# Row sums by way of DRAM, value tiles copied in SBUF, and late sums folded on VectorE, in the first layer of a two-layer backbone

## What is computed

```python
m = jax.nn.silu(cond) @ w_mod + b_mod            # shift, scale, gate
h = x * (1.0 + sc) + sh
q, k, v, z = jnp.split(h @ w_in[l], 4, axis=-1)
s = jnp.concatenate([s_loc.reshape(b, h, GRID_W, n_win), s_ctx], axis=-1)
p = jax.nn.softmax(s, axis=-1).astype(v.dtype)
y = einsum('bhwij,bhiwjd->bhwd', p_loc, v_win) + einsum('bhwc,bhcd->bhwd', p_ctx, vc)
out = (y * jax.nn.silu(z)) @ w_out[l]
x_new = _layer_norm(DEEPNORM_ALPHA * x + (1.0 + g) * out, ln_g[l], ln_b[l])
```

## Time and profile before

| | |
|---|---|
| median of 3 runs | 1820.04 us (1819.77 to 1820.56) |
| the profiled execution | 1819.72 us, span 1817.9 us |
| PE busy | 1781.4 us (98%), 10525 matmuls |
| PE weight loads busy | 1541.5 us (85%) |
| DVE busy | 1260.0 us (69%), 2268 instructions |
| ACT busy | 925.2 us (51%), 1680 instructions |
| POOL busy | 268.3 us (15%) |
| granted PE clock | 0.998 of full |
| DMA | 124.92 MB, 69 GB/s |

### The profile page before, as it was taken

How to read it: one execution, slowest core, us unless ns; L and a number is a source line. 1 busy time by engine, 2 the same in 40 slices (tenths; PEclk the granted TensorE clock), 3 DMA queues, 4 the chain that set the end, 5 groups by cost and what they waited for, 6 DMA issues and landing times. The chain is left out here.

```text
span 1817.9 us, 30832 instructions
## 1 busy us (share of the span) xinstructions
PE 1781.4 (98%) x10525; PEld 1541.5 (85%) x10525; DVE 1260.0 (69%) x2268; ACT 925.2 (51%) x1680; POOL 268.3 (15%) x219
## 2 busy tenths in 40 slices
PE   7999999999999999989999999999999999999998
PEld 4898989888888888878878988888888888898886
DVE  6677776867677767774877576584848485756758
ACT  2555555565555656570045556464737465554500
POOL 3200000000000000165441010100001010102951
PEclk9999999999999999999999999999999999999999
DMA  9312121212222221234511010101010000101343
GB/s 347 87 52 86 45 85 40 79 54 75 61 75 61 58 78 49 88 96 162 189 70 36 13 46 4 42 12 46 12 35 23 35 23 14 44 12 45 101 154 119
DMA packets 73663, 124.92 MB, mean 69 GB/s; under 512 B 41312, under 2 KB 41472, under 8 KB 73488
## 3 DMA queue, kind: packets, MB, share of 16 engines
q1 hardware_dynamic: 68496, 106.48, 18.3%
q0 software_dynamic: 2384, 8.39, 1.7%
q10 hardware_dynamic: 2736, 9.44, 1.3%
HBM read 106.54 MB, written 17.73 MB: 68 GB/s over the span
## 5 line engine op out<-in xcount | busy, mean ns | idle before, releaser
L522 PE MATMUL acc<-h_hi,w_hi 128*128 128x512 f32 (+1 forms) x1408 | 524.5, 373 | 2.3 <-DVE w_lo L505 1.1
L522 PE MATMUL acc<-h_hi,w_lo 128*128 128x512 f32 (+1 forms) x1408 | 508.7, 361 | 0.0
L522 PE MATMUL acc<-h_lo,w_hi 128*128 128x512 f32 (+1 forms) x1408 | 508.1, 361 | 0.0
L522 PEld LDWEIGHTS acc<-h_hi,w_lo 128*128 128x128 f32 x1408 | 265.5, 189 | 41.5
L522 PEld LDWEIGHTS acc<-h_hi,w_hi 128*128 128x128 f32 x1408 | 265.9, 189 | 39.1 <-DVE h_lo L447 3.6
L522 PEld LDWEIGHTS acc<-h_lo,w_hi 128*128 128x128 f32 x1408 | 266.4, 189 | 33.6
L1649 DVE TENSOR_REDUCE stats<-acc 128x1 f32<-128x1280 f32 x128 | 189.6, 1487 | 43.5 <-PE acc L1756 42.8
L1559 ACT ACTIVATE far_prob<-acc,stats 128x1280 f32<-128x1280 f32 x128 | 170.1, 1329 | 28.3 <-DVE stats L1649 26.6
L1566 ACT ACTIVATE far_pt<-acc 128x512 f32<-128x512 f32 (+1 forms) x192 | 101.0, 526 | 162.6 <-PE acc L1765 159.2
L1756 PE MATMUL acc<-k_dup,q_stack 128*128 128x512 f32 (+1 forms) x768 | 176.9, 367 | 1.8 <-ACT far_prob L1559 0.4
L1160 ACT ACTIVATE near_pt_hi<-acc 128x384 fp32r<-128x384 f32 (+1 forms) x208 | 110.4, 531 | 122.6 <-PE acc L1347 104.4
(11 more groups left out here) (207 smaller groups left out, 2961.7 us busy)
## 6 DMA issues: line engine op xcount, KB each, us to landing
w_raw<-in_w_in SPq DMA_DIRECT2D x64, 512.0 KB, 3.3
near_late_slots<-in_w_mod SPq DMA_DIRECT2D x64, 256.0 KB, 2.6
w_raw<-in_w_out SPq DMA_DIRECT2D x16, 512.0 KB, 3.3
w_raw<-y_t POOLq DMA_DIRECT2D x14, 448.0 KB, 5.2
y_t<-y SPq DMA_DIRECT2D x7, 640.0 KB, 3.1
modulation_rows<-in_w_scale SPq DMA_DIRECT2D x8, 512.0 KB, 6.4
modulation_rows<-in_w_mod SPq DMA_DIRECT2D x8, 512.0 KB, 6.4
out_rows<-in_x SPq DMA_DIRECT2D x8, 512.0 KB, 4.7
```

The source lines that it names most:

```text
L522: mm = nc.tensor.matmul(m.bank(self.bank_of(j, c), w), wt[:, b % 2, k, :], ht[:, k, t0:t0 + w], start=(k == 0 and i == 0), stop=(k == KT - ...
```

## The change

- **Row sums.** `repeat_factors`, `spread_factors` and the ring are gone. ScalarE's queue stores the four reciprocals of each query, 128 x 4 single numbers, in a DRAM array `factor_rows` (`store_factors`, in the even steps at the place of `repeat_factors`), and loads them back in the next odd step with two DMAs, one for each head, that spread a row of 256 numbers over 64 partitions (`load_factors`, between `exp` and `take_low`). `scale_gate` reads SBUF. It and `gate_y` stand together at the end of even steps from 4 on, a step later than before; those of the last column at the end of the chunk.
- **Values.** `turn_v` has three turns (4, 4, 2 tiles), each token once. The tiles that start at cells 1 and 3 are put together from the others by DMAs in SBUF from GpSimd's queue (`move_values`, two for each of two shifts); the values product waits for them from step 3 on.
- **Late sums.** At the chunk's end VectorE transposes the accumulators in blocks of 32 x 32 and adds within each block (`fold`); the next chunk's front has one matmul of 128 x 32 by 32 columns behind product 4 (`reduce`). Rows are stored a chunk later, in pieces of 512 numbers, and what reads them (gains, `cols_in`) follows: `cols_in` with eight DMAs instead of two. In the last chunk the row is computed as before.
- Part n of the probabilities uses bank 4 + n % 2.

```diff
-        self.v_turns = [(b // 2, [b * BAND_TOKENS + s0 * CELL for s0 in K_STRIP0]) for b in range(BANDS)]
-        self.v_turns += [(2, [SEQ, SEQ + P])]
+        self.v_turns = [(g, range(t0, t0 + w, P)) for g, (t0, w) in enumerate(GROUPS)]
...
+    def fold(self, v, c):
+        v.wait_ge(self.summed, CREDIT + c * 2 * KT + 2 * KT)
+        for cnd in range(2):
+            self.nc.vector.transpose(self.slots[cnd], self.acc[cnd]).then_inc(self.folded, 1)
+        v.wait_ge(self.reduced, CREDIT + c * 1 + 1)
+        for cnd in range(2):
+            v.wait_ge(self.folded, CREDIT + c * 4 + 4 + cnd + 1)
+            self.nc.vector.reduce_sum(self.part[:, cnd * 16:(cnd + 1) * 16],
+                                      self.slots[cnd].rearrange("p (b n) -> p b n", n=FOLD), AX).then_inc(self.folded, 1)
...
     def reduce(self, pe, c, bank):
-        pe.wait_ge(self.summed, CREDIT + c * 2 * KT + 2 * KT)
-        for cnd in range(2):
-            mm = self.nc.tensor.matmul(self.m.psum[0:2, bank, :], self.m.pick[:, cnd, :], self.acc[cnd],
-                                       start=(cnd == 0), stop=(cnd == 1))
-        mm.then_inc(self.reduced, 1)
+        pe.wait_ge(self.folded, CREDIT + c * 4 + 4)
+        self.nc.tensor.matmul(self.m.psum[0:FOLD, bank, 0:FOLD], self.part, self.m.quads[:, :], start=True, stop=True)\
+            .then_inc(self.reduced, 1)
...
+    def move_values(self, pool, c, shift):
+        pool.wait_ge(self.v_ready, CREDIT + c * 2 * self.NV + 4)
...
+        pool.dma_start(moved[0:P - start], tiles[start:P, 0]).then_inc(self.v_moved[shift], 16)
+        pool.dma_start(moved[P - start:P], tiles[0:start, 1]).then_inc(self.v_moved[shift], 16)
...
         self.product(pe, c, 4)
+        pe.wait_ge(self.evac, CREDIT + c * self.evacs + 3)
+        late.reduce(pe, c, 7)
         self.turn_v(pe, c, 2)
-        self.turn_v(pe, c, 3)
         self.product(pe, c, 5)
-        self.turn_v(pe, c, 4)
...
+    def factors_in(col):
+        return factor_rows[col].rearrange("i q -> q i")
+
+    def factors_out(col, head):
+        row = factor_rows[col, 2 * head:2 * head + 2, :].rearrange("r q -> (r q)")
+        return bass.AP(row.tensor, row.offset, [[0, HD], [1, 2 * P]])
...
+                    def store_factors(col):
                         act.wait_ge(recip_done, CREDIT + c * COLS + (col + 1))
+                        act.dma_start(factors_in(col), of_column(4), allow_slow_non_contiguous=True).then_inc(factors_stored, 16)
+
+                    def load_factors(col):
+                        act.wait_ge(factors_stored, CREDIT + (c * COLS + (col + 1)) * 16)
+                        for head in range(2):
+                            act.dma_start(near.factors[col % 2][64 * head:64 * head + 64, :], factors_out(col, head))\
+                                .then_inc(factors_loaded, 16)
...
                         if step % 2 == 0 and step:
-                            repeat_factors(step // 2 - 1)
+                            store_factors(step // 2 - 1)
                         if step < NU:
                             exp(2 * step)
                         if step % 2 and step >= 3:
+                            load_factors(step // 2 - 1)
                             take_low(step // 2 - 1)
...
-                    act.wait_ge(spread, CREDIT + (c + 1) * COLS)
-                    late.take_row(act, c, 1 if last else 7)
                     take_low(COLS - 1)
+                    load_factors(COLS - 1)
...
-                        v.wait_ge(spread, CREDIT + c * COLS + (col + 1))
-                        nc.vector.tensor_tensor(gate, units[2 * col].of_result(ring_bank(ring.index((SCALE, col)))[:, 0:2 * P]), gate,
-                                                ALU.mult).then_inc(gate_scaled, 1)
+                        v.wait_ge(factors_loaded, CREDIT + (c * COLS + (col + 1)) * 32)
+                        nc.vector.tensor_tensor(gate, units[2 * col].of_result(near.factors[col % 2]), gate, ALU.mult).then_inc(gate_scaled, 1)
...
-                        if step % 2 and step >= 3:
-                            gate_y(step // 2 - 1)
-                        if step % 2 == 0 and step:
-                            scale_gate(step // 2 - 1)
+                        if step % 2 == 0 and step >= 4:
+                            scale_gate(step // 2 - 2)
+                            gate_y(step // 2 - 2)
...
                     sum_y(COLS - 1)
+                    if not last:
+                        late.fold(v, c)
+                    scale_gate(COLS - 1)
                     gate_y(COLS - 1)
```

## The result

| | before | after |
|---|---|---|
| median of 4 runs | 1819.91 us (1819.77 to 1820.56) | 2040.89 us (2036.67 to 2045.59) |
| ratio | | 1.1214, interval 1.1198 to 1.1231 |
| span of the profiled execution | 1817.9 us | 2039.1 us |
| granted PE clock | 0.998 | 0.952 |

The change costs 221 us. The forecast was 1819.5 with a range to 1834: the time lies 207 us outside it. First the page of the changed kernel: busy time of each engine, and the span in 40 slices.

The account below looks back on a forecast made before the run. TensorE was taken as the bound, with VectorE's order already binding in odd steps. Seven chunks at +0.07 us (+0.5), first chunk -0.55 and last -0.5 gave together -0.5 us: 1819.5 us, range 1806 to 1834.

Parts of the forecast that it names:

- The store's landing: Store of the reciprocals to DRAM: taken as 2.5 us, between 1.8 (a bias DMA) and 5.8 (`sub_gain`).
- For columns 0 to 3 a whole step of 6 us hides it: Round trip through DRAM, 4.6 us in all, was to cost nothing except for the last column at the chunk's end.
- Rival 1: Store plus load exceed 5.8 us and end the chunk: up to 2.1 us a chunk, 1834 us; chance 0.27.
- the third turn: `turn_v(2)`, near the chunk's boundary, waits for VectorE's `values_lo(0)`: starts 0.55 us behind TensorE.
- DMA issues on ScalarE: Two load issues ahead of `take_low` lie under `exp`: 0.05 us in each of three steps, +0.15 a chunk.
- steps 3, 5 and 7: Odd steps of a chunk's 0 to 10, each charged 0.05 us for DMA issues, bounds 0 and 0.85.
- step 9: Steps 8 and 9: `exp` followed by two DMA issues, `take_low` and `sum_y` reach the values later, +0.35 us.
- Rival 3: ScalarE runs dry before each DMA; issues delay `take_low` by 0.85 in four steps, +3.0 us a chunk, 1841; chance 0.07.
- `gate_y` in the even steps: `gate_y` ahead of the next `row_max` adds 0.45 us there; terms of +0.26, +0.45 and +0.35 a chunk.
- The chunk's end: Removed `reduce` matmuls and later transposes, less new waits for VectorE and its 2.5 us fold: -0.94 us a chunk.
- The turns: `turn_v` makes 10 transposes instead of 18, TensorE saving 0.6 and 0.2 us a chunk; moves hidden.
- The sum: All terms of a chunk added: +0.07 us, seven times +0.5.

Follow-up runs that it names:

- e5: The changed kernel with each of the 512 single numbers stored 64 bytes apart in DRAM, loads reading weight rows: 1830.74 us.
- e7: The changed kernel storing only one of four reciprocals per query, 128 single numbers side by side in DRAM, loads reading weight rows: 1996.14 us.
- e9: The changed kernel with the DRAM array ordered by query, so the 512 single numbers are written one behind the other: 1977.3 us.
- e3: The changed kernel storing 128 pieces of 16 bytes instead of 512 of 4, factors reaching the gate in a wrong order: 1829.87 us.
- e4: The changed kernel with reciprocals transposed on VectorE and stored as 16 pieces of 128 bytes, all computed: 1834.16 us, ratio 1.0088.
- e13: e4 with the loads issued at the end of the odd steps instead of ahead of `take_low`: 1824.52 us, ratio 1.0029.
- e11: The kernel before the change with the moved values alone, row sums and late sums as before: 1811.76 us, ratio 0.9956.
- e8: The changed kernel storing 512 pieces of 32 bytes from an unchanging tile, loads reading weight rows: 1830.2 us.

## Why the prediction was wrong, point by point

- **The store's landing: the step that failed.** "I take 2.5, nearer the bias rows": 8.5 to 11.6 was measured, 9.45 in the median. The bounds of 1.8 and 5.8 came from the earlier trace rows, and all three rows there are loads into SBUF; none writes single neighbours to DRAM. The upper bound was too low, and the sum's only check on it was the chunk's end. The runs e5 and e7 name the cause: the neighbours, not the number of pieces. The prediction quoted the Trainium skill, VectorE: DVE Perf Modes, The three transpose paths, on copies that transpose by their strides; the page says it of copies whose innermost stride at the destination is large, a condition that the prediction left out. Here such strides alone cost nothing (e5 has them, 2.3 us), and e9, which writes one number behind the other, is slow without them. So it pointed to the right rival for a reason that the runs do not bear out.
- **"For columns 0 to 3 a whole step of 6 us hides it": wrong, and the dearer half.** I had named who waits for the landing only at the chunk's end. In the odd steps the loads' wait stands on ScalarE's queue ahead of `take_low`, and for that wait `sum_y` and the values: every us beyond the step stops all three engines. Rival 1 had the right side and the right transfer, but it saw only the chunk's end, at 2.1 us a chunk. There the third turn waits 43.8 / 7 = 6.3 us a chunk more than in e3, and the odd steps, which it left out, cost twice that. Measured against e3 the whole is 122.34 - 95.84 = 26.5 us a chunk.
- **How 26.5 us come out of a landing that is 7 us later than forecast.** The spans of the changed kernel and e3 differ by 2039.1 - 1827.9 = 211.2 us, with the same 10369 matmuls. 66.4 of it are busy time (1823.4 against 1757.0), 144.8 idle. The waits for `sum_y` grew by 125.9 - 24.1 = 101.8, those of the third turn by 47.9 - 4.1 = 43.8. The busy part is the clock. Taken in stretches of 1 us up to 1050 us, TensorE is busy for some 147 us at half the clock, in e3 for none; half of that, 73 us, is an estimate of what it costs, near the 66.4. Behind the wait of 5.00 us that ended at 384.35 a matmul of 512 columns takes 0.63 instead of 0.39 (0.43 instead of 0.23 from start to start), and the granted clock is half, that is 1.2 GHz (timeline of TensorE, then shares by stretch, the seventh number being the clock):

```profile
385.79 0.63 PE L558 MATMUL acc<-h_lo,w_hi 128*128 128x512 f32 x1
...
423.17 0.39 PE L558 MATMUL acc<-h_hi,w_hi 128*128 128x512 f32 x1
```

```profile
384.00:388.00 4.00, 3.65 (x11) 3.08 (x12) 1.63 (x4) 1.16 (x4) 0.00 (x0) 0.50 0.34 73
388.00:392.00 4.00, 4.00 (x32) 4.00 (x31) 2.63 (x9) 2.52 (x5) 0.00 (x0) 0.91 0.07 1
```

The prediction said nothing of what an idle TensorE costs once it resumes.
- **DMA issues on ScalarE: 0.15 us a chunk forecast, 1.2 measured** (e4 to e13), within the bounds of 0 to 0.85 each. The 0.15 covered steps 3, 5 and 7; step 9's issues stood in its 0.35. The earlier trace rows shows that the queue handles a semaphore event ahead of the engine; from that I took that issues do so too. They begin only when `exp` begins, and 1.10 us do not fit under its 0.88 (320.20 to 321.08). Rival 3 had the right delay, that of `take_low`, at more than twice the price, but not the way it comes about: ScalarE doesn't run dry before an issue, the issue runs beside `exp` and outlasts it. The rule of the Trainium skill that the prediction set beside it (Advanced Engine Details and Errata, Sequencer Loop) made these terms 0, as the prediction read it; the measurement decides against that.
- **`gate_y` in the even steps: 1.06 forecast (0.26, 0.45 and 0.35), 1.1 measured** (0.77 net, and 0.33 that one more `gate_y` costs at the third turn). The sum agrees, in part by luck: the 0.35 of step 9 counted the issues too, and no run measured the three places one by one.
- **The chunk's end, with a store that lands in time: right.** The fold takes 2.5 us (423.47 to 425.94), as forecast, and the third turn waits 0.59 (4.1 over 7, e3) against 0.55. The last values product gains 1.81 - 1.41 = 0.40 against 0.33; the new matmul takes 0.25. In the changed kernel the loads land so late that the fold ends 7.9 us ahead of `scale_gate`, which is what the prediction named as the sign of rival 1:

```profile
423.47 1.31 DVE L398 STREAM_TRANSPOSE near_late_slots<-near_late_acc 128x512 f32<-128x512 f32 x2
424.70 1.24 DVE L402 TENSOR_REDUCE stats<-near_late_slots 128x16 f32<-128x512 f32 x2
433.85 0.42 DVE L1290 TENSOR_TENSOR gate<-near_factors,gate 128x256 f32<-128x256 f32 x1 [7.91 <-DMA near_factors<-factor_rows]
```

- **The turns: right.** Ten transposes instead of eighteen were to give 0.8 us a chunk; e11 gives 0.96. That the moves are hidden is right too.
- **The sum.** With a store that lands in time a chunk was to take 0.07 us more than before; e3 takes 95.84 - 94.43 = 1.41 more. The issues explain some 1.05 of the difference of 1.34 (1.2 for 0.15). Some 0.3 us stay unexplained.

What stays open: why neighbours in DRAM land so late. That the memory takes small writes to one stretch one behind the other would fit the table, but it is only a guess: no run shows the memory at work. How large such a stretch is stays open too.

## What to carry to other kernels

A store with a semaphore that an engine's queue waits for is priced by its landing, and in these runs the landing of small pieces went by what lay beside them in DRAM: keep pieces at 16 bytes or more, or apart, and turn them on an engine first where that is cheap. Count what stands behind the waiting instruction in its engine's order at every place, not only where the path ends, and put the wait behind work that is ready. A saving of 1 us on the busiest engine is no gain if three places of its partners grow by 0.35 to 0.45 us.

## What the runs showed of the hardware

- Stores of single 4-byte numbers from SBUF to neighbouring places in DRAM land after 7.0 to 13.2 us, with 128 or 512 of them; 64 bytes apart, 512 land in 2.3 us. In the one store that was looked at, the DMA engines are through with the pieces 1.3 us after the issue (369.90 to 371.2), and move nothing until 377. The Trainium skill, DMA: Bandwidth & Descriptors, Anatomy of one DMA — SWDGE (gpsimd) path, says of DMAs from GpSimd's queue that the semaphore moves only when the memory has confirmed the last byte, and that this can take surprisingly long for DRAM. The stores here come from ScalarE's queue. The trace agrees in kind; the page's figure of about 2 us for the fixed part agrees with 1.9 to 2.3 in e3, e5 and e8, and not with the 9.45 of the change.
- A DMA issue on ScalarE's queue started 0.08 us after the start of the activation ahead of it (320.28 in e3, 369.90 in the changed kernel), not before; two last 1.10 us, and what they outlast that activation by is seen in the next one (0.34).
- TensorE's clock did not fall behind every wait. In the one of 5.00 us it fell while TensorE still stood: 1.00 to 381 us, 0.50 from 382 to 388. Two others were as long as each other, 3.50 (to 401.56) and 3.48 us (to 417.69). After the first the clock was still full when TensorE resumed and halved some 0.8 us later, after the second it stayed full:

```profile
382.00:383.00 1.00, 0.00 (x0) 0.00 (x0) 0.00 (x0) 0.38 (x1) 0.00 (x0) 0.50 0.96 287
...
401.00:402.00 1.00, 0.45 (x3) 0.45 (x4) 0.94 (x3) 1.00 (x4) 0.00 (x0) 1.00 0.54 60
...
403.00:404.00 1.00, 1.00 (x6) 1.00 (x6) 1.00 (x2) 0.38 (x1) 0.00 (x0) 0.50 0.81 173
...
417.00:421.00 4.00, 1.90 (x12) 1.48 (x12) 2.88 (x7) 0.92 (x3) 0.00 (x0) 1.00 0.12 15
```
